# The first norm's gain moved into the projections' weights, its roots applied behind the projections, in a two-block transformer kernel

## The reference

```python
def rms_norm(x, gain):
    y = x * lax.rsqrt(jnp.mean(x * x, axis=-1, keepdims=True) + RMS_EPS)
    return y * gain
...
h = rms_norm(x, pre_mix_norm)
proj = h @ w_in                       # 1024 x 2560
q, k, v_a, u, v_s = jnp.split(proj, [512, 1024, 1536, 2048], axis=-1)
q = partial_rotary(q.reshape(B, S, 8, 64), positions)
k = partial_rotary(k.reshape(B, S, 8, 64), positions)
attn = dilated_mixture_attention(q, k, v_a)
sgu = spatial_gating(u, v_s, ...)     # gelu of u and of v_s first
```

## Time and profile before

| | us |
|---|---|
| median of 3 runs | 1813.76 (1810.85 to 1814.03) |
| profiled execution, its own time | 1813.32 |
| its span, first to last instruction | 1811.5 |
| TensorE busy | 1776.8 |
| first transpose starts | 8.61 |
| first product starts | 13.69 |
| first product of block `k` starts | 38.55 |

### The profile page before, as it was taken

The page is one execution under the profiler, slowest core; times in us unless marked ns, Lnnn a source line. Parts: engine busy times, 40 slices in busy tenths (PEclk is TensorE's granted clock), DMA queues, the critical chain, the costliest instruction groups (busy, mean ns, idle before and its releaser), DMA issues.

```text
span 1811.5 us, 24680 instructions
## 1 busy us (share of the span) xinstructions
PE 1776.8 (98%) x9586; PEld 1449.5 (80%) x9586; DVE 1114.1 (62%) x1763; ACT 834.3 (46%) x1593; POOL 336.4 (19%) x404
## 2 busy tenths in 40 slices
PE   7999999999999999999999999999999999999998
PEld 7767898888888877878878787767788998888886
DVE  7556643233345787887768746677556357574847
ACT  5346532222224555554555644554434445352535
POOL 1403000000000046254462640000020012112120
PEclk9999999999999999999999999999999999999999
DMA  7212333332322453352433444233443248849482
GB/s 256 72 58 63 101 110 116 93 93 93 94 93 75 152 143 128 119 149 97 160 131 123 142 147 164 86 105 118 139 151 130 69 148 189 236 101 259 117 206 70
DMA packets 140419, 230.85 MB, mean 127 GB/s; under 512 B 27264, under 2 KB 59456, under 8 KB 139664
## 3 DMA queue, kind: packets, MB, share of 16 engines
q1 hardware_dynamic: 118944, 166.70, 29.0%
q0 software_dynamic: 20496, 60.10, 12.5%
q10 hardware_dynamic: 864, 2.49, 0.3%
HBM read 216.54 MB, written 12.71 MB: 127 GB/s over the span
## 4 chain that ended last, share of the span: by engine, by line
PE 80%; DVE 11%; ACT 3%; DMA 3%; issue 2%; POOL 1%; SPq 0%; DVEq 0%; ACTq 0%; POOLq 0%
PE m L2135 14%; PE m L2137 13%; PE m L2136 13%; PE m L2146 6%; PE m L2148 6%; PE m L2147 6%; PE s L2298 4%; DVE lo L1396 3%; DMA raw<-in_w_up_dram 2%; PE m L2245 2%; PE m L2244 2%; PE m L2243 2%; PE s L2294 1%; PE m L2270 1%; PE m L2272 1%
## 5 line engine op out<-in xcount | busy, mean ns | idle before, releaser
L2135 PE MATMUL m<-hH,hi 128*128 128x512 f32 (+1 forms) x1392 | 529.4, 380 | 3.2 <-DVE hL L1426 1.8
L2137 PE MATMUL m<-hH,lo 128*128 128x512 f32 (+1 forms) x1392 | 509.1, 366 | 0.0
L2136 PE MATMUL m<-hL,hi 128*128 128x512 f32 (+1 forms) x1392 | 508.3, 365 | 0.0
L1396 DVE TENSOR_TENSOR lo<-raw,hi 128x1024 fp32r<-128x1024 f32 x267 | 335.8, 1269 | 189.7 <-ACT hi L916 189.4
L916 ACT ACTIVATE hi<-raw 128x1024 fp32r<-128x1024 f32 x267 | 276.1, 1050 | 200.8 <-DMA raw<-in_w_up_dram 52.9
L2135 PEld LDWEIGHTS m<-hH,hi 128*128 128x128 f32 x1392 | 262.6, 189 | 47.7 <-DVE hL L1426 2.4
L2137 PEld LDWEIGHTS m<-hH,lo 128*128 128x128 f32 x1392 | 262.4, 189 | 43.4
L2136 PEld LDWEIGHTS m<-hL,hi 128*128 128x128 f32 x1392 | 262.9, 189 | 39.0
L2146 PE MATMUL m<-hi,hH 128*128 128x512 f32 (+1 forms) x320 | 133.8, 418 | 1.6 <-DVE lo L1396 1.6
L2148 PE MATMUL m<-hi,hL 128*128 128x512 f32 (+1 forms) x320 | 122.5, 383 | 0.0
L2147 PE MATMUL m<-lo,hH 128*128 128x512 f32 (+1 forms) x320 | 122.4, 382 | 0.0
(11 more groups left out here) (330 smaller groups left out, 3032.6 us busy)
## 6 DMA issues: line engine op xcount, KB each, us to landing
raw<-in_w_in_dram SPq DMA_DIRECT2D x72, 512.0 KB, 3.6
wq<-in_w_down_dram POOLq DMA_DIRECT2D x40, 512.0 KB, 10.0
hn<-scr_cs_dram POOLq DMA_DIRECT2D x32, 512.0 KB, 4.1
raw<-in_w_up_dram SPq DMA_DIRECT2D x32, 512.0 KB, 5.7
wq<-in_w_down_dram SPq DMA_DIRECT2D x24, 512.0 KB, 7.7
raw<-in_w_gate_dram SPq DMA_DIRECT2D x44, 256.0 KB, 2.8
raw<-in_w_up_dram SPq DMA_DIRECT2D x44, 256.0 KB, 3.1
raw<-in_w_down_dram SPq DMA_DIRECT2D x22, 512.0 KB, 4.2
```

Source lines behind the costliest of these rows:

```text
L1396: e.tensor_tensor(d, r, h.bitcast(F32), ALU.subtract).then_inc(s_lo, 1)
L2135: e.matmul(bank, wh[:, kk, c], h[:, k, q], start=k == 0, stop=False)
L2136: e.matmul(bank, wh[:, kk, c], l[:, k, q], start=False, stop=False)
L2137: x = e.matmul(bank, wl[:, kk, c], h[:, k, q], start=False, stop=k == kt - 1)
```

## The change

The product (x·root·gain) @ w is written as root·(x @ (gain·w)).

- **Gain.** The host lays it out as 128 x 8, so that `GC` (4 KB) has on each partition the gains of its eight weight rows. For units 0 to 19 (all of `w_in`) the rounding is `HI = round(RAW * GC)` and the remainder `LO = RAW * GC - HI`, each in two instructions of 512 columns instead of one of 1024.
- **Turns.** TensorE transposes `X` itself. Tiles 0 and 1 are loaded in half tiles: first halves at the very start (tile 0's behind the identity), second halves from ScalarE's queue, behind its rounding of turn 0. The order of the turns is 0, 2, 1, 3. Tiles 2 and 3 are loaded by SyncE, which waits for the third and fourth turn; weight unit 3 and all that follows stand behind that. Units 1 and 2 no longer wait.
- **Roots.** ScalarE squares the tiles in slots 6 to 9 (`N_S1`), VectorE's `inverse` makes reciprocals and diagonal matrices of them in slots 7 to 10. TensorE transposes the four diagonal matrices in slot 12, which leaves in bank `side[0]` each token's root on all partitions; VectorE multiplies `RS` and `RC` with it in slot 14, so that the rotary embedding scales q and k. v, u and the gates get the root as the evacuation's scale.

```diff
 for t in range(4):
-    N_S0.append(-1), N_S1.append(-1), N_HN.append(-1), N_TR.extend([(-1, -1), (-1, -1), (2, 3), (4, 5)][t])
+    N_S0.append(-1), N_S1.append(6 + t), N_HN.append(7 + t), N_TR.extend([(-1, -1), (-1, -1), (2, 3), (4, 5)][t])
+SEAT = {1: 2, 2: 1}
...
 # sync_program
-            e.dma_start(X[:, 0, :], A["x"][0, 0:128, :]).then_inc(s_x[0], 16)
             e.dma_start(CST[:, 0:128], A["consts"][:, 0:128]).then_inc(s_id, 16)
+            e.dma_start(X[:, 0, 0:512], A["x"][0, 0:128, 0:512]).then_inc(s_x[0], 16)
...
-                    if b.u0 + u in (1, 2):
-                        o.wait_ge(s_x[b.u0 + u - 1], 16)
+                    if b.u0 + u == NRAW:
+                        for t in range(2, 4):
+                            o.wait_ge(s_ntr, t + 1)
+                            e.dma_start(X[:, t, :], A["x"][0, 128 * t:128 * t + 128, :]).then_inc(s_x[t], 16)
...
 # scalar_program, split_weights
+                if j < BLK["wo0"].u0:
+                    o.wait_ge(s_gain[0], 16)
+                    for kk in range(2):
+                        k = 2 * (j % 4) + kk
+                        x = e.activation(d[:, kk, :], r[:, kk, :], ACT.Copy, scale=GC[:, k:k + 1])
+                    x.then_inc(s_hi, 1)
+                    return
...
-                    e.activation(V[:, i, :], bank[:, :], ACT.Copy).then_inc(s_eva, 1)
+                    o.wait_ge(s_inv, 4)
+                    e.activation(V[:, i, :], bank[:, :], ACT.Copy, scale=st(ST_N[i] + 2)).then_inc(s_eva, 1)
...
-            e.dma_start(X[:, 1, :], A["x"][0, 128:256, :]).then_inc(s_x[1], 16)
-            e.dma_start(G[0][:, :], A["pre_mix_norm"][0].partition_broadcast(128)).then_inc(s_gain[0], 16)
+            e.dma_start(X[:, 1, 0:512], A["x"][0, 128:256, 0:512]).then_inc(s_x[1], 16)
+            e.dma_start(GC[:, :], A["pre_mix_norm"]).then_inc(s_gain[0], 16)
             prepare_root()
-            norm_squares(0, 1)
-            for t in range(2, 4):
-                e.dma_start(X[:, t, :], A["x"][0, 128 * t:128 * t + 128, :]).then_inc(s_x[t], 16)
-            root(ST_N[1], (s_sq1, 1), s_nrs, True)
+            norm_round(0)
+            for t in range(2):
+                e.dma_start(X[:, t, 512:1024], A["x"][0, 128 * t:128 * t + 128, 512:1024]).then_inc(s_x[t + 2], 16)
+            norm_round(2)
             split_weights(0)
-            norm_round(0)
+            split_weights(1)
             norm_round(1)
-            norm_round(2)
             norm_round(3)
-            split_weights(1)
-            norm_squares(2, 1)
             split_weights(2)
-            norm_squares(3, 1)
             split_weights(3)
...
 # vector_program
+                if j < BLK["wo0"].u0:
...
+                        x = e.scalar_tensor_tensor(out=d[:, kk, :], in0=r[:, kk, :], scalar=GC[:, k:k + 1], in1=h[:, kk, :].bitcast(F32), op0=ALU.mult, op1=ALU.subtract)
+                    x.then_inc(s_lo, 1)
...
+            def inverse(n):
+                r = st(ST_N[n] + 2)
+                o.wait_ge(s_nrs, n + 1)
+                e.reciprocal(r, r).then_inc(*o.own())
+                o.settle()
+                o.wait_ge(s_id, 16)
+                e.tensor_scalar(PT[1][:, 128 * n:128 * n + 128], ident, 0.0, r, ALU.mult, ALU.add).then_inc(s_inv, 1)
...
                 if g == 11:
...
-                    e.tensor_scalar(RS[:, :], RS[:, :], CST[:, C_SF:C_SF + 1], None, ALU.mult).then_inc(s_rsf, 1)
+                if g == 14:
+                    o.wait_ge(s_cwt, 1)
+                    e.scalar_tensor_tensor(out=RS[:, :], in0=RS[:, :], scalar=CST[:, C_SF:C_SF + 1], in1=side[0][:, :], op0=ALU.mult, op1=ALU.mult).then_inc(s_rsf, 1)
+                    o.wait_ge(s_rt, 3)
+                    e.tensor_tensor(RC[:, :], RC[:, :], side[0][:, :], ALU.mult).then_inc(s_rsf, 1)
...
-            o.wait_ge(s_x[1], 16)
-            e.tensor_tensor_reduce(HN[1][:, :], X[:, 1, :], X[:, 1, :], 1.0, 0.0, ALU.mult, ALU.add, st(ST_N[1] + 1)).then_inc(s_sq1, 1)
-            norm_scale(0)
-            o.wait_ge(s_sq1, 1)
-            norm_scale(1)
             norm_rest(0)
-            norm_rest(1)
+            norm_rest(2)
             split_weights(0)
-            norm_rest(2)
-            norm_rest(3)
             split_weights(1)
-            norm_scale(2)
+            norm_rest(1)
+            norm_rest(3)
             split_weights(2)
-            norm_scale(3)
             split_weights(3)
...
 # tensor_program
-                o.wait_ge(s_nlo, 2 * n0 + 4 * h + (3 if u < 2 else 4))
+                o.wait_ge(s_nlo, 2 * n0 + 4 * h + (4 if u >= 2 else 2 if b.name == "q" and h == 0 else 3))
...
+                    if g == 12:
+                        claim("side", 0)
+                        o.wait_ge(s_inv, 4)
+                        for t in range(4):
+                            x = transpose(side[0][:, 128 * t:128 * t + 128], PT[1][:, 128 * t:128 * t + 128])
+                        x.then_inc(s_cwt, 1)
+                        read["side", 0] = (s_rsf, 2)
```

More of the change, by code:

```diff
@@ L547, in build @@
         s_wd, WD_FROM = s_os, 64
-        s_wq, WQ_FROM = s_x, 16
-        s_sq1 = sem("s_sq1")
+        s_wq, WQ_FROM = s_x, [16, 16, 32, 32]
+        s_inv = sem("s_inv")
         main = [ctx.enter_context(nc.psum_tensor(f"m{i}", [128, 512], F32)) for i in range(4)]
@@ L560, in build @@
         EPS = sb("EPS", [128, 1])
-        sb("gap", [128, 84])
+        GC = sb("GC", [128, 8])
+        sb("gap", [128, 76])
         RAW = [sb(f"raw{i}", [128, 2, 512]) for i in range(NRAW)]
@@ L695, in load_gain @@
                 g, s = G[i % 2], s_gain[i % 2]
-                if i in (2, 6, 8):
-                    o.wait_ge(s_hn, {2: 8, 6: 16, 8: 24}[i])
+                if i in (6, 8):
+                    o.wait_ge(s_hn, {6: 8, 8: 16}[i])
                 if i == 3:
@@ L923, in norm_squares @@
                     if h:
-                        o.wait_ge(s_x[n] if n < 4 else s_mem[n - 12], 16)
+                        if n < 2:
+                            o.wait_ge(s_x[n], 16)
+                            o.wait_ge(s_x[n + 2], 16)
+                        else:
+                            o.wait_ge(*((s_x[n], 32) if n < 4 else (s_mem[n - 12], 16)))
                         root(c, square(X[:, n, :] if n < 4 else MEMX[:, t, :], st(c + 1)), s_nrs, True)
@@ L966, in evacuate @@
                 elif n == "v":
-                    e.activation(V[:, i, :], bank[:, :], ACT.Copy).then_inc(s_eva, 1)
+                    o.wait_ge(s_inv, 4)
+                    e.activation(V[:, i, :], bank[:, :], ACT.Copy, scale=st(ST_N[i] + 2)).then_inc(s_eva, 1)
                 elif n == "u":
                     o.wait_ge(s_wt, 2)
-                    e.activation(MIX[:, i, 512:1024], bank[:, :], ACT.Gelu).then_inc(s_eva, 1)
+                    e.activation(MIX[:, i, 512:1024], bank[:, :], ACT.Gelu, scale=st(ST_N[i] + 2)).then_inc(s_eva, 1)
                 elif n[:2] == "gu":
@@ L1092, in mixture @@
                     o.wait_ge(s_bank, b.e0 + t + 1)
-                    e.activation(VS[:, t, :], main[t][:, :], ACT.Gelu).then_inc(s_eva, 1)
+                    e.activation(VS[:, t, :], main[t][:, :], ACT.Gelu, scale=st(ST_N[t] + 2)).then_inc(s_eva, 1)
                 for x in SE_AT.get(g, ()):
@@ L1171, in convolutions @@
                     o.wait_ge(s_xsv, 16)
-                    o.wait_ge(s_hn, 24)
+                    o.wait_ge(s_hn, 16)
                     if i >= 2:
@@ L1395, in split_weights @@
                     d, r, h = LO[j % NHL][:, :, :], RAW[j % NRAW][:, :, :], HI[j % NHL][:, :, :]
-                e.tensor_tensor(d, r, h.bitcast(F32), ALU.subtract).then_inc(s_lo, 1)
+                if j < BLK["wo0"].u0:
+                    o.wait_ge(s_gain[0], 16)
+                    for kk in range(2):
+                        k = 2 * (j % 4) + kk
+                        x = e.scalar_tensor_tensor(out=d[:, kk, :], in0=r[:, kk, :], scalar=GC[:, k:k + 1], in1=h[:, kk, :].bitcast(F32), op0=ALU.mult, op1=ALU.subtract)
+                    x.then_inc(s_lo, 1)
+                    return
+                e.tensor_tensor(d, r, h.bitcast(F32), ALU.subtract).then_inc(s_lo, 1)
+            def inverse(n):
[5 more added lines that the diff above has]
+                e.tensor_scalar(PT[1][:, 128 * n:128 * n + 128], ident, 0.0, r, ALU.mult, ALU.add).then_inc(s_inv, 1)
             def norm_scale(n):
+                if n < 4:
+                    inverse(n)
+                    return
                 t = n % 4 if n < 12 else n - 12 if n < 14 else (n - 14) % 4
@@ L1440, in residual_add @@
                 o.settle()
-                o.wait_ge(s_hn, 8 if m < 4 else 16)
+                if m >= 4:
+                    o.wait_ge(s_hn, 8)
                 if m < 4:
@@ L1507, in evacuate @@
                     t = 2 * q + i % 2
[L1509 removed]
+                    o.wait_ge(s_hn, 36)
                     if (t, h) in added:
@@ L2303, in norm_turn @@
                 o.wait_ge(s_id, 16)
-                o.wait_ge(s_hn, i + 1)
```

(13 more changed lines are left out.)

23 lines of the change are left out of this document (11 added, 12 removed).

## The result

The changed kernel takes 1817.3 us (median of 20 runs, 1815.2 to 1820.8) against 1813.7 us (20 runs, 1810.9 to 1815.3): the ratio is 1.0022, with a 95% interval of 1.0016 to 1.0028. (A ratio here is estimated over all runs of both kernels, and is not the quotient of the two medians.) It is slower by 3.6 us by the medians, and 1817.3 lies past the upper end of the forecast's range, 1816.4. The profiled execution took 1816.08 us (before 1813.32).

What follows compares the result with a forecast made beforehand. The prediction took TensorE, busy 98% of the span, as the bound. Its terms, -2.9 + 0.63 + 1.7 + 0.44 = -0.1 us, against a median of 1813.76 gave a forecast of 1813.6 us, range 1810.4 to 1816.4.

Steps and rivals of the forecast that it cites:

- What costs nothing, and its cover: Weight halves add about 0.1 us on ScalarE, 0.2 on VectorE, twenty times, at no cost; the first scores' 1.5 us wait stays.
- Rival (d): Blocks of v and behind: longer remainders delay the attention's chain on VectorE; plus 1 us, 1814.6; chance 0.1.
- The start: Ahead of the first product: it starts at 10.8 us instead of 13.69, 2.9 us earlier; bounds 10.0 and 12.0.
- The clock at the start: First products: half speed for 1.25 us, until the clock rises at 12.05, costs 0.63 us; bounds 0 and 1.5.
- The roots: Slot 12: TensorE, there at 30.55, waits 1.7 us for the fourth diagonal, seen at 32.25; bounds 0 and 3 us.
- Four transposes: Slot 12: the four added transposes of the roots' diagonals cost 0.44 us.
- (a): Slot 12: the roots are in time, their chain 1.7 us shorter than added up; 1811.9; chance 0.2.
- (b): Slot 12: late constants and spatial weights hold up the angles; at 26.8 the wait is 4.1 us; 1816.0; chance 0.1.
- (c): Start: second halves behind the weights are seen only at 12.5, so the -2.9 us falls away; 1816.5; chance 0.1.

Runs made afterwards that it cites:

- plain units: The changed kernel with weight units 4 to 19 rounded and subtracted without the gain, in one instruction on each engine: 1813.4 us, ratio 1.0005.
- the busy wait: The changed kernel with eighteen unread transposes on TensorE ahead of the second scores: 1816.4 us, ratio 1.0017.
- the later units: The changed kernel with units 12 to 15 rounded and subtracted in slots 42, 44, 46 and 48: 1814.0 us, ratio 1.0005.
- the busy start: The changed kernel with eighteen unread transposes on TensorE between turns 2 and 1: 1818.4 us, ratio 1.0029.
- late roots: The changed kernel with the four diagonals' transposes in slot 14 instead of 12 and the scaling in slot 15: 1815.8 us, ratio 1.0013.
- the early halves: The changed kernel with the second halves issued first by ScalarE, and turns 1 and 3 ahead of weight unit 1: 1815.3 us, ratio 1.0010.
- the kernel before with halves: The kernel before with rounding and remainder of units 4 to 19 in two halves each, by a scale of one: 1815.8 us, ratio 1.0016.
- one part: The kernel before with the remainder of units 4 to 19 in one multiply-and-subtract instruction, by a scale of one: 1812.2 us, ratio 0.9997.

## Why the prediction was wrong

**The step that failed** stands in "What costs nothing, and its cover". The halves were priced by their durations alone, 0.1 us a unit on ScalarE and 0.2 on VectorE, and then put at nothing, since units 4 and 5 have time. Two things were wrong in that. First, they are not off the path: at the unit whose remainder stands ahead of the first shuffle of `K`, ScalarE's 0.28 (1.33 against 1.05) and VectorE's 0.18 (1.41 against 1.23) add 0.46 us on the way to the first softmax. Second, VectorE's price holds only where it works alone. Beside GpSimd's embedding the two remainders last 3.48 and 3.47 us instead of 2.14 and 2.31, and the embedding 0.73 us longer. The same paragraph said that the wait of 1.5 us stays because it hangs on k: it became 2.7, and the experiments show that even its 1.5 were this contention, for with the units moved away they vanish. Rival (d) had the place and the direction ("longer remainders delay the attention's chain") but 1 us and a chance of 0.1; it was 1.2 us in one piece and 1.5 of clock behind it, which the sum had at nothing. The trace before showed it: the largest remainder lasts 2.31 us beside a median of 1.23.

The Trainium skill (SBUF — State Buffer, "Who interferes with whom") says that a VectorE instruction with two inputs in SBUF and a GpSimd instruction that reads SBUF exclude each other, and that the second blocks for the whole instruction. By this each instruction more is one more block. The traces agree: one instruction pays 0.9 to 1.1 us (2.14 and 2.31 against 1.23 for the subtraction, 2.20 and 2.31 against 1.28 with a scale); two pay 2.07 (3.48 against 1.41).

**The start.** The forecast put the first product at 10.8, it came at 11.62. The mis-sized term is the landing of the second halves: about 10.0 and 10.6 instead of 8.95 and 9.6, so their turns start at 10.00 and not at 9.05. The order was as forecast, weights first. But by 7 us 1.61 MB had passed and not 1.75, the last weights passed between 8.5 and 9 us instead of by 8.0, and from 9 us on ScalarE's queue moved 0.25 MB in a microsecond where the sum had 0.4.

**The clock at the start.** The mechanism was right (the rise comes late because of the hole), the term was mis-sized: +1.40 measured, 0.63 forecast, 1.5 the bound. The low level lasted past 14.5, not to 12.05. The run with the hole filled shows the cause: products of 280 ns from 11.4 on.

**The roots.** The wait was there, 0.5 us for the 1.7 of the forecast. TensorE's own lateness explains the difference: it was at the transposes at 32.27 and not at 30.55. The diagonals were ready at 32.73, forecast 32.15. That they were late by so little is two errors that partly cancel: the angles, which stand ahead of the last two diagonals, had a CAST of 0.42 us where the earlier trace rows had 1.41, while everything began later with turn 7 (21.60 instead of 20.0). In the other kernels with the roots in slot 12 the wait was 0.5 to 1.2 us, and with the start at full clock 2.7. The forecast left out what moves it: GpSimd's masking, which starts at 23.2 us in the changed kernel and at 24.0 to 24.3 in the kernels with plain units, the busy wait and the later units, can hold up the first diagonal. In these four profiles the second reciprocal starts 0.1, 0.4, 0.8 and 0.7 us after its root is ready, and the wait is 0.5, 0.7, 1.2 and 1.1.

**Four transposes**: 0.44 in slot 14, without a wait, as forecast; in slot 12 they and the wait cost 1.16 us together, for the 2.14 of the forecast. **Rivals (a), (b), (c)** did not come as they were told: the second halves were used at 10.00, the constants and spatial weights set GpSimd off at 23.22 (before 22.88), before the 24.4 from which (b) counts. But late spatial weights do cost, by another way than (b)'s: through the diagonal that the masking holds up.

Up to block `k` the terms were -2.07, +1.40 and +1.16, forecast -2.9, +0.63 and +2.14: +0.47 measured, -0.1 predicted. That this is near is partly luck, since each term is off by 0.8 to 1 us and they cancel, and partly the luck of one execution: the three kernels with the same start and the roots in the same slot stand at +1.02, +1.46 and +1.51 ahead of the second scores. What put the forecast outside its range came behind: +1.19 and +1.49.

**What stays open.** The matched products explain 3.1 us at 644 us and the profiled executions differ by 2.8; the medians differ by 3.6 (by the ratio 4.0, interval 2.9 to 5.1). The spread of the start from execution to execution, up to 1.1 us in the four profiles above, is large enough for the rest. Why the same wait of 2.7 us was followed by the low clock in three profiled executions (the changed kernel, the one with the busy start, the one with late roots) and not in two (the early halves and the kernel before with halves) is not settled. The mean granted clock, on record for every run, hints at how often it happens: it is 0.997 or less in 19 of 20 runs of the changed kernel and in 7 of 11 of the kernel before with halves, against 9 of 103 of the kernel before and 1 of 11 with plain units. In the kernel with halves these seven runs have a median of 1816.8 us and the four others 1814.7, which fits a wait of 1.2 us in every run and the clock's fall in most of them. The mean doesn't say where in the run the clock fell, and near 660 us it falls too, in ten of the fourteen profiled executions: in the changed kernel with units 12 to 15 later 4 of 11 runs are at 0.997 although no wait at the scores is left.

## What to carry to other kernels

The number of instructions counts where two engines exclude each other: splitting one VectorE operation into two cost 0.2 us where it ran alone and 1.2 to 1.3 where GpSimd worked beside it, so look for the stretches in which the same operation already lasts longest before you split it. And a wait can't be called "stays" by its releaser's name: follow the chain behind it (softmax, embedding, shuffle, remainder) to the work that is late. A gain at the start of a kernel is kept only if what is due next (the roots, ScalarE's evacuation of q, the weights' arrival) comes earlier too; the fix here was to move four weight units out of the embedding's stretch, which pays 2 us without the change as well.

## What the runs showed of the hardware

- VectorE beside GpSimd, each with operands in SBUF: 1024 columns in one instruction 2.14 and 2.31 us for 1.23 (subtraction) and 2.20 and 2.31 for 1.28 (with a scale); two of 512 columns 3.48 for 1.41. Other kinds too: the angles' CAST 1.41 us before, beside GpSimd's masking (22.88 to 25.29), and 0.42 in the changed kernel, behind it; a diagonal of 128 columns 1.29 us beside it in the changed kernel and 2.42 with the busy start, and 0.29 alone.
- ScalarE's DMAs behind weights of SyncE's queue: two of 256 KB, issued at 6.0 and 6.3 us, moved 0.01 MB until 8, then 0.26 and 0.25 MB in a microsecond each, and landed 4.0 and 4.3 us after their issue. In the earlier trace rows two of 512 KB, issued from 6.70 on, moved next to nothing until 10.
- TensorE after standing still for 2.7 us at the second scores: the low clock from about 1 us behind its return until 4 us behind it in three executions, no fall in two; after 1.5 us (the kernel before, plain units, one part) no fall. From 40 us to the wait it did the same in all five: products without a gap at 1.00. Near 660 us, where it stands still for part of 655 to 660 us in every kernel (busy 2.29 of 5 us before), the clock fell in ten of fourteen.
- With TensorE filled with transposes whose results nobody reads, products lasted 280 ns from 11.4 us on at the start, and the clock stayed at 1.00 behind the gap at the scores, in one profiled execution each.
